# Delta layer of a two-layer decoder: GpSimd inverts blocks of 32 on 128 partitions, and one merging level fewer stays on TensorE

## The chip, the cores and the metric

The kernel runs on one core of a Trainium2 chip. The metric is the device time of one execution in microseconds (us), as the median of several executions. The profile is of one execution, taken by the hardware profiler.

## What is computed

Two layers over 1024 tokens of width 1024, each with a norm, one input projection, a mixer, a gate and one output projection. The change touches the mixer of the first layer only, a gated delta rule with 8 heads. The kernel works on chunks of 128 tokens (the reference on 64, with the same result). Cut to what matters:

```python
def gated_delta_rule(q, k, v, g, beta):
    ...
    lower = jnp.where(strict, jnp.einsum("bhnid,bhnjd->bhnij", k_beta, k) * decay, 0.0)
    rhs = jnp.concatenate([v * beta[..., None], k_beta * jnp.exp(g)[..., None]], axis=-1)
    sol = lax.linalg.triangular_solve(lower + jnp.eye(C, dtype=f32), rhs,
                                      left_side=True, lower=True, unit_diagonal=True)
    u, w = sol[..., :DV], sol[..., DV:]
    qk = jnp.einsum("bhnid,bhnjd->bhnij", q, k) * decay

    def step(state, inp):
        q_c, k_c, u_c, w_c, g_c, qk_c = inp
        v_new = u_c - jnp.einsum("bhck,bhkv->bhcv", w_c, state)
        o = (jnp.einsum("bhck,bhkv->bhcv", q_c * jnp.exp(g_c)[..., None], state)
             + jnp.einsum("bhij,bhjv->bhiv", qk_c, v_new))
        ...
```

The kernel needs the inverse of `lower + I` for each of the 8 chunks (tiles of 128x128) of each head.

## The kernel before

The delta layer is the function `delta_heads`. It runs a `body(m, n, p)` nine times: in each, head n is projected, convolved and prepared while head m = n - 1 goes through its merging levels and its chain of 8 states. The first body has no head m, the last one no head n. I number the bodies 0 to 8 by their n. A body is 36 slots, and each engine has its own program of the same slots, in order. On TensorE (PE) a slot s holds a piece of head m's chain, then 8 matmuls of 128x512 of the projection (`three_passes`, L373), then the small products of head n, and last the merging level of head m if there is one in this slot. In the last body only a part of a gate projection, 4 matmuls per slot, is left of the projection (`GATE_PARTS`).

The inverse of a tile is made in two ways. GpSimd (POOL) inverts the diagonal blocks of size BLK = 16 by forward substitution, all 64 blocks of a head at a time, a block on each partition (`invert_blocks`, L604 to L629): two instructions for each of 15 columns, a product (L619) and a subtraction (L622), each waiting for the one before. Then LEVELS = 3 merging levels join blocks of 16 to 32, 64 and 128. A level takes two slots of PE: in the first, two products `first` (L955), copied by ScalarE (ACT) to `bc` (L669); in the second, four products `lev` (L962, L964; two in the last level), applied by VectorE (DVE) to `zx1` (L1017) or, at the end, to `zf` (L1019). The four pairs of tiles start 6 slots apart, the first at slot LEVEL0 = 1. The masked inputs of all levels of a pair are made by one POOL instruction (`um`, L591).

The path of the blocks between layouts goes through DRAM, by DMAs that SyncE (SP) issues in its own order. At slot 21 (`BLOCKS_OUT`) SP stores the tiles u (L553), waits, and loads the blocks to `bd` (L557). At slot 34 (`INVERSE_BACK`) it waits for POOL (L564), stores the two results (L567, L568), waits for both (L569) and loads the four parts of `zx` (L572). The first two of these four hold the first pair of tiles, and PE waits for them at the first level of the next body (L952). In SP's order there follow the last store of head m's output (L562, slot 36) and, at slot 3 of the next body, the load of that head's second weight unit, 512 KB (L534). ACT waits for this load in its slot 2 (`split_high`, L639), ahead of its own later slots. In a body in which ACT also has the copy `bc` in slot 2, that copy stands ahead of `split_high`.

Of the kernel before, what the change touches and what calls it, by code (L numbers as in the profile page):

```python
# [25 lines left out]
P = 128  # L26
S = 1024
D = 1024
T = S // P
# [12 lines left out]
EXP_LN = "natural_log_exp_and_others"  # L42
BIG = 1e30
ARG_MAX = 44.0
BLK = 16
NB = P // BLK
LEVELS = 3
BLOCK_STEP = BLK * (P + 1)
TILE_STEP = NB * BLOCK_STEP

# [294 lines left out]
SLOTS = 36  # L345
UNITS = 6
HALVES = 2 * UNITS
LEVEL0 = 1
DECAYS = (12, 15)
CHAIN0 = 7  # L350
K_TURNS = (22, 34)
# [25 lines left out]
def delta_heads(nc, g, weights, proj, o_turned):  # L377
# [5 lines left out]
    with ExitStack() as ctx:  # L383
        m_ = Mem(nc, ctx, "a")
# [12 lines left out]
        cols = m_.sb("cols", [P, 7, T, H])  # L397
        hc = m_.sb("hc", [P, 2, 7, T])
        hw = m_.sb("hw", [P, 2, CONV, 4])
        bd = m_.sb("bd", [NB * T, BLK, BLK])  # L400
        bx = m_.sb("bx", [NB * T, BLK, BLK])
        bt = m_.sb("bt", [NB * T, (BLK // 2) ** 2])
        dec = m_.sb("dec", [P, T, P])
        um = m_.sb("um", [P, 2, LEVELS, P])
        bc = m_.sb("bc", [P, 2, P])
# [15 lines left out]
        u_dram = nc.dram_tensor("u_tiles", [T * TILE_STEP], F32, kind="Internal").ap()  # L421
        inv_dram = nc.dram_tensor("inverse_tiles", [2, T * TILE_STEP], F32, kind="Internal").ap()
# [5 lines left out]
        def as_blocks(flat):  # L428
            return (flat.rearrange("(p x) -> p x", x=BLOCK_STEP)[:, 0:BLK * P]
                    .rearrange("p (j i) -> p j i", i=P)[:, :, 0:BLK])  # L430

        step = m_.ps("step", [P, 2, DV])
        new = m_.ps("new", [P, DV])
# [18 lines left out]
        inv_out, inv_zero = sem("inv_out"), sem("inv_zero")  # L452
        back = [sem("back_first"), sem("back_rest")]
        bstep = sem("bstep")
# [73 lines left out]
        @block.sync  # L528
        def _(sp):
            def load(n, j):  # L530

                sp.wait_ge(w_low, n * UNITS + j)
                sp.sem_inc(carrier, 1)
                sp.dma_start(raw[:, slot_of(j)], weights.w[:, bass.ds(col_of(n, j), P)]  # L534
                             .rearrange("(k p) c -> p k c", p=P)).then_inc(w_landed[slot_of(j)], 16)


            sp.wait_ge(zx_zero, 1)
            for c in range(2):
                sp.dma_start(as_tiles(inv_dram[c]), zx[:, :, c, :]).then_inc(inv_zero, 16)  # L540
            sp.wait_ge(inv_zero, 32)

            def body(m, n, p):
                for s in range(DELAYED):
                    if n is not None and s < SLOTS and s % 6 == 3:
                        j = s // 6 + 1
                        if j < UNITS:
                            load(n, j)
                        elif not (isinstance(n, int) and n == H - 1):
                            load(n + 1, 0)  # L550
                    if n is not None and s == BLOCKS_OUT:
                        sp.wait_ge(ut, n * 4 + 2)
                        sp.dma_start(as_tiles(u_dram), u[:, :, :]).then_inc(blocks_out, 16)  # L553
                        if not (isinstance(n, int) and n == 0):
                            sp.wait_ge(inv_out, n * 32)
                        sp.wait_ge(blocks_out, n * 16 + 16)
                        sp.dma_start(bd[:, :, :], as_blocks(u_dram)).then_inc(blocks_in, 16)  # L557
                    if m is not None and (s - CHAIN0 - 8) % 3 == 0 and 0 <= (s - CHAIN0 - 8) // 3 < T:
                        t = (s - CHAIN0 - 8) // 3
                        sp.wait_ge(og_s, m * T + (t + 1 + T))  # L560
                        dst = o_turned[bass.ds(m * DV, DV), t * P:(t + 1) * P].rearrange("(c p) n -> p c n", p=P)
                        sp.dma_start(dst, og[:, :, :]).then_inc(o_stored, 16)  # L562
                    if n is not None and s == INVERSE_BACK:
                        sp.wait_ge(blocks_inv, n * 2 + 2)  # L564

                        sp.wait_ge(lv_s, n * (LEVELS * T // 2) + 1)
                        sp.dma_start(as_blocks(inv_dram[0]), bd[:, :, :]).then_inc(inv_out, 16)  # L567
                        sp.dma_start(as_blocks(inv_dram[1]), bx[:, :, :]).then_inc(inv_out, 16)  # L568
                        sp.wait_ge(inv_out, n * 32 + 32)  # L569
                        for part, tiles in enumerate((slice(0, 2), slice(2, T))):  # L570
                            for c in range(2):
                                sp.dma_start(zx[:, tiles, c, :], as_tiles(inv_dram[c])[:, tiles]  # L572
                                             ).then_inc(back[part], 16)

            heads(sp, body)
            sp.wait_ge(o_stored, 16 * (1 + H * T))

        @block.gpsimd
        def _(pool):
            pool.memset(zx[:, :, :, :], 0.0).then_inc(zx_zero, 1)  # L580
            pool.wait_ge(cols_s, 1)

            def body(m, n, p):
                if n is not None:
                    columns_and_taps(n, p)
                if m is not None:
                    for b in range(T // 2):

                        pool.wait_ge(first_mm, m * (LEVELS * T // 2) + (LEVELS * b + 1))
                        pool.wait_ge(ut, m * 4 + 2)  # L590
                        pool.tensor_tensor(um[:, :, :, :], spread(u[:, 2 * b:2 * b + 2, :], 2, LEVELS),  # L591
                                           spread(g.level_mask[:, :, :], 1, 2), ALU.mult).then_inc(um_s, 1)
                if n is not None:
                    invert_blocks(n)

            def columns_and_taps(n, p):

                pool.wait_ge(og_s, n * T)
                pool.tensor_copy(hc[:, p], cols[:, :, :, bass.ds(n, 1)].rearrange("p a t o -> p a (t o)")
                                 ).then_inc(hc_s, 1)  # L600
                for c, tile in ((0, n + H), (1, n + 0), (2, n * 2 + 2 * H), (3, n * 2 + (2 * H + 1))):
                    pool.tensor_copy(hw[:, p, :, c:c + 1], g.conv[:, :, bass.ds(tile, 1)]).then_inc(hc_s, 1)

            def invert_blocks(n):  # L604

                if not (isinstance(n, int) and n == 0):
                    pool.wait_ge(inv_out, n * 32)
                pool.sem_inc(carrier, 1)
                pool.memset(bx[:, :, :], 0.0).then_inc(bstep, 1)
                pool.wait_ge(bstep, n * (2 * BLK) + 1)  # L610
                pool.sem_inc(carrier, 1)
                pool.tensor_copy(bx[:, :, :].rearrange("t j i -> t (j i)")[:, 0:BLK * BLK:BLK + 1],
                                 g.ones[0:NB * T, 0:BLK]).then_inc(bstep, 1)
                pool.wait_ge(blocks_in, n * 16 + 16)
                for j in range(BLK - 1):
                    pool.wait_ge(bstep, n * (2 * BLK) + (2 + 2 * j))
                    rows, width = BLK - 1 - j, j + 1
                    prod = bt[:, 0:rows * width].rearrange("t (i c) -> t i c", c=width)
                    pool.tensor_tensor(prod, spread(bd[:, j, j + 1:BLK], 2, width),  # L619
                                       spread(bx[:, j, 0:width], 1, rows), ALU.mult).then_inc(bstep, 1)  # L620
                    pool.wait_ge(bstep, n * (2 * BLK) + (3 + 2 * j))
                    pool.tensor_tensor(bx[:, j + 1:BLK, 0:width], bx[:, j + 1:BLK, 0:width], prod,  # L622
                                       ALU.subtract).then_inc(bstep if j < BLK - 2 else blocks_inv, 1)

                pool.wait_ge(blocks_inv, n * 2 + 1)
                pool.sem_inc(carrier, 1)
                pool.tensor_copy(bd[:, :, :], bx[:, :, :].rearrange("t i c -> t c i")).then_inc(blocks_inv, 1)
                pool.wait_ge(blocks_inv, n * 2 + 2)
                pool.sem_inc(bstep, 1)  # L629

            heads(pool, body)

        @block.scalar
        def _(act):
# [26 lines left out]
            def body(m, n, p):  # L661
                pm = 1 - p
                for s in range(DELAYED):
                    if m is not None:
                        b, k = divmod(s - LEVEL0 - 1, 6)
                        if 0 <= b < T // 2 and k % 2 == 0:
                            use = LEVELS * b + k // 2
                            act.wait_ge(first_mm, m * (LEVELS * T // 2) + (use + 1 + 1))
                            act.activation(bc[:, :, :], first[:, :, :], ACT.Copy).then_inc(first_c, 1)  # L669
# [101 lines left out]
        def _(pe):  # L771
# [18 lines left out]
            def body(m, n, p):  # L790
# [23 lines left out]
                for s in range(SLOTS):  # L814
# [124 lines left out]
                    if m is not None:  # L939

                        b, k = divmod(s - LEVEL0, 6)
                        if 0 <= b < T // 2:
                            level, second = divmod(k, 2)
                            use = LEVELS * b + level
                            x = zx[:, 2 * b:2 * b + 2] if level == 0 else zx1[:, :, :, :]
# [24 lines left out]
        def _(dve):  # L970
# [33 lines left out]
            def body(m, n, p):  # L1004
                pm = 1 - p
                for s in range(DELAYED):
                    if m is not None:
                        b, k = divmod(s - LEVEL0 - 2, 6)
                        if 0 <= b < T // 2 and k % 2 == 0:
                            level = k // 2  # L1010
                            use = LEVELS * b + level
                            x = zx[:, 2 * b:2 * b + 2] if level == 0 else zx1[:, :, :, :]
# [1191 lines left out]
```

## Time and profile before

| | |
|---|---|
| median of 3 executions | 2395.16 us |
| the profiled execution | 2399.3 us |
| its span, first to last instruction | 2397.6 us |
| PE busy | 2308.8 us (96%) |
| PEld busy (weight loads, beside PE) | 1922.3 us (80%) |
| DVE busy | 1423.4 us (59%) |
| ACT busy | 1264.1 us (53%) |
| POOL busy | 245.5 us (10%) |

Busy times are sums over the whole span, so they don't say what bounds one stage. The delta layer takes the first 955 us of the span. All times in the rows further down are counted from the start of the span. In the timelines, an entry is start, duration, engine, line, operation, output<-input and a count, with idle time and its releaser in square brackets; consecutive matmuls overlap, so that the time a matmul costs is the distance to the start of the next, not its duration.

### The profile page before, as it was taken

Reading aid. Unit: us, or ns where it says so; the run is one execution under the profiler, and the core shown is the slowest. Engines: PE = TensorE matmul, PEld = TensorE weight load, DVE = VectorE, ACT = ScalarE, POOL = GpSimd, SP = SyncE. Lnnn points to the kernel's source line nnn. Section 1 sums busy time; section 2 is a strip of 40 time slices with the busy share of each in tenths; the row PEclk is TensorE's granted clock in tenths of the full one; section 3 lists DMA queues with packets and bytes.
Section 4 is the critical chain, followed back from the end, with each engine's and each line's share of the span. In section 5 each row is a group of like instructions: output and inputs, shape, how many; then the busy total and the mean of one; then the engine's idle time right before and its main releaser. Section 6 shows DMA issues by size and latency. Waiting matters only on the chain. (4 is left out here: it accounts for less than half of the span.)

```text
span 2397.6 us, 35088 instructions
## 1 busy us (share of the span) xinstructions
PE 2308.8 (96%) x11486; PEld 1922.3 (80%) x11486; DVE 1423.4 (59%) x2614; ACT 1264.1 (53%) x2565; POOL 245.5 (10%) x387
## 2 busy tenths in 40 slices
PE   7999999999999997999999999999999999999869
PEld 6788888887888876778788888888888888888757
DVE  5665756575757563786663827456382745638155
ACT  5556556565556654555445455454554445455433
POOL 1202121211212120830000000000000000000000
PEclk9999999999999999999999999999999999999989
DMA  4123030212121221978112112111211211111077
GB/s 135 38 58 79 23 88 24 78 37 66 39 62 50 54 63 30 292 265 283 54 28 63 36 35 70 35 53 32 56 35 35 70 35 53 38 51 36 19 240 268
DMA packets 279550, 186.26 MB, mean 78 GB/s; under 512 B 72140, under 2 KB 258660, under 8 KB 279428
## 3 DMA queue, kind: packets, MB, share of 16 engines
q1 hardware_dynamic: 279428, 184.73, 26.2%
q8 instruction: 65, 1.06, 0.2%
q14 instruction: 57, 0.47, 0.1%
HBM read 157.23 MB, written 27.46 MB: 77 GB/s over the span
## 5 line engine op out<-in xcount | busy, mean ns | idle before, releaser
L373 PE MATMUL b_front<-g_h_hi,wb_w_hi 128*128 128x512 f32 x1280 | 511.8, 400 | 3.0 <-PEq L1275 3.0
L373 PE MATMUL b_front<-g_h_hi,wb_w_lo 128*128 128x512 f32 x1280 | 511.4, 400 | 0.0
L373 PE MATMUL b_front<-g_h_lo,wb_w_hi 128*128 128x512 f32 x1280 | 510.3, 399 | 0.0
L373 PE MATMUL a_proj<-g_h_hi,wa_w_hi 128*128 128x512 f32 x784 | 323.3, 412 | 3.2 <-ACT a_acc L720 1.7
L373 PE MATMUL a_proj<-g_h_lo,wa_w_hi 128*128 128x512 f32 x784 | 323.0, 412 | 0.0
L373 PE MATMUL a_proj<-g_h_hi,wa_w_lo 128*128 128x512 f32 x784 | 316.8, 404 | 0.0
L373 PEld LDWEIGHTS b_front<-g_h_hi,wb_w_hi 128*128 128x128 f32 x1280 | 241.7, 189 | 51.6 <-issue 3.3
L373 PEld LDWEIGHTS b_front<-g_h_hi,wb_w_lo 128*128 128x128 f32 x1280 | 241.5, 189 | 50.6
L373 PEld LDWEIGHTS b_front<-g_h_lo,wb_w_hi 128*128 128x128 f32 x1280 | 241.7, 189 | 49.2
L1864 ACT ACTIVATE b_acc<-b_front,g_gains 128x512 f32<-128x512 f32 x96 | 66.2, 689 | 285.4 <-DVE b_qk L2123 206.0
L2020 DVE TENSOR_TENSOR wb_w_lo<-wb_raw,wb_w_hi 128x1024 fp32r<-128x1024 f32 x79 | 95.9, 1214 | 140.0 <-ACT wb_w_hi L1825 140.0
L373 PEld LDWEIGHTS a_proj<-g_h_hi,wa_w_hi 128*128 128x128 f32 x784 | 148.3, 189 | 33.9 <-issue 3.2
L373 PEld LDWEIGHTS a_proj<-g_h_lo,wa_w_hi 128*128 128x128 f32 x784 | 148.4, 189 | 29.8 <-issue 1.0
L373 PEld LDWEIGHTS a_proj<-g_h_hi,wa_w_lo 128*128 128x128 f32 x784 | 148.1, 189 | 27.9
L1080 DVE SCALAR_TENSOR_TENSOR a_acc<-a_x_raw,a_hw,a_acc 128x512 f32<-128x512 f32 x192 | 145.7, 759 | 6.8
L2088 DVE TENSOR_TENSOR b_sq_lo<-b_sg,b_sq_hi 128x512 fp32r<-128x512 f32 x96 | 66.2, 690 | 80.7 <-ACT b_sq_hi L1869 80.7
L591 POOL TENSOR_TENSOR a_um<-a_u,g_level_mask 128x768 f32<-128x768 f32 x32 | 60.9, 1902 | 426.8 <-PE a_first L955 426.6
L669 ACT ACTIVATE a_bc<-a_first 128x256 f32<-128x256 f32 x96 | 36.5, 380 | 127.6 <-PE a_first L955 119.1
L1017 DVE TENSOR_TENSOR a_zx<-a_zx,a_lev 128x512 f32<-128x512 f32 x64 | 43.9, 685 | 79.2 <-PE a_lev L964 79.2
L2123 DVE TENSOR_TENSOR b_qk<-b_acc,b_sg 128x512 f32<-128x512 f32 x96 | 90.0, 938 | 0.1
L725 ACT ACTIVATE a_sg<-a_sg 128x512 f32<-128x512 f32 x92 | 57.0, 620 | 56.2 <-DVE a_sg L1084 56.0
L1897 ACT ACTIVATE b_v<-b_side 128x512 f32<-128x512 f32 x48 | 28.6, 596 | 107.8 <-PE b_side L2006 107.8
(273 smaller groups left out, 4565.6 us busy)
## 6 DMA issues: line engine op xcount, KB each, us to landing
wb_raw<-in_b_w_in_dram SPq DMA_DIRECT2D x80, 512.0 KB, 3.9
p_w_raw<-in_a_w_out_dram SPq DMA_DIRECT2D x64, 512.0 KB, 4.2
wa_raw<-in_a_w_in_dram SPq DMA_DIRECT2D x48, 512.0 KB, 4.2
p_w_raw<-in_b_w_out_dram SPq DMA_DIRECT2D x32, 512.0 KB, 4.2
a_out<-a_og SPq DMA_DIRECT2D x64, 128.0 KB, 1.8
p_a_raw<-a_out SPq DMA_DIRECT2D x64, 128.0 KB, 5.1
a_zx<-inverse_tiles SPq DMA_DIRECT2D x16, 384.0 KB, 4.5
u_tiles<-a_u SPq DMA_DIRECT2D x8, 512.0 KB, 3.2
```

The lines of the kernel that those rows point to most:

```text
L373: last = pe.matmul(out, w[:, k, :], a[:, k, ks], start=(n == 0), stop=(n == 23))
L591: pool.tensor_tensor(um[:, :, :, :], spread(u[:, 2 * b:2 * b + 2, :], 2, LEVELS), spread(g.level_mask[:, :, :], 1, 2), ALU.mult).then_inc( ...
L669: act.activation(bc[:, :, :], first[:, :, :], ACT.Copy).then_inc(first_c, 1)
L725: act.activation(sg[:, q % 2], sg[:, q % 2], ACT.Exp).then_inc(sigs, 1)
L1017: dve.tensor_tensor(zx1[:, :, :, :], x, lev[:, :, :, :], ALU.subtract).then_inc(lv_s, 1)
L1080: ins = dve.scalar_tensor_tensor(acc[:, half], src, w, acc[:, half], ALU.mult, ALU.add)
L1864: act.activation(acc[:, half], proj[half][:, :], ACT.Copy, scale=r.gains[:, gain:gain + 1]).then_inc(rope, 1)
L1897: act.activation(v[:, c // 2, (c % 2) * TH:(c % 2 + 1) * TH, :], side[:, :].rearrange("p (t c) -> p t c", t=TH), ACT.Copy).then_inc(v_kept, 1)
L2020: dve.tensor_tensor(w_lo[slot_of(j)][:, :, :], raw[:, slot_of(j)], w_hi[slot_of(j)][:, :, :].bitcast(F32), ALU.subtract).then_inc(w_low, 1)
L2088: dve.tensor_tensor(sq_lo[:, :], sg[:, q % 2], sq_hi[:, :].bitcast(F32), ALU.subtract).then_inc(sq_low, 1)
L2123: dve.tensor_tensor(out, a, b_, ALU.mult).then_inc(qkn, 1)
```

## The change

BLK goes from 16 to 32 and LEVELS from 3 to 2: POOL inverts 32 blocks of 32 per head, and the level that joined 16 to 32 is gone. To use all 128 partitions, the columns of a block's inverse are dealt to four groups of 32 partitions, 8 columns (`PART`) to each; `bd` is loaded four times, once for each group. The substitution has 31 columns instead of 15, with a width of at most 8. The results are stored by eight DMAs instead of two. LEVEL0 goes from 1 to 3: a pair's levels take slots 3 to 6 of its six instead of 1 to 6, so that the last level stays where it was.

```diff
-BLK = 16
+BLK = 32
 NB = P // BLK
-LEVELS = 3
+LEVELS = 2
+PARTS_OF_BLOCK = P // BLK
+PART = BLK // PARTS_OF_BLOCK
...
-LEVEL0 = 1
+LEVEL0 = 3
...
-        bd = m_.sb("bd", [NB * T, BLK, BLK])
-        bx = m_.sb("bx", [NB * T, BLK, BLK])
-        bt = m_.sb("bt", [NB * T, (BLK // 2) ** 2])
+        bd = m_.sb("bd", [P, BLK, BLK])
+        bx = m_.sb("bx", [P, BLK, PART])
+        bt = m_.sb("bt", [P, (BLK - PART) * PART])
+        bxt = bd[:, 0:PART, :]
...
+        def part_of(tile, q):
+
+            return tile[q * NB * T:(q + 1) * NB * T]
+
+        def columns(q):
+            return slice(q * PART, (q + 1) * PART)
...
-                        sp.dma_start(bd[:, :, :], as_blocks(u_dram)).then_inc(blocks_in, 16)
+                        for q in range(PARTS_OF_BLOCK):
+                            sp.dma_start(part_of(bd, q), as_blocks(u_dram)).then_inc(blocks_in, 16)
...
-                        sp.dma_start(as_blocks(inv_dram[0]), bd[:, :, :]).then_inc(inv_out, 16)
-                        sp.dma_start(as_blocks(inv_dram[1]), bx[:, :, :]).then_inc(inv_out, 16)
-                        sp.wait_ge(inv_out, n * 32 + 32)
+                        for q in range(PARTS_OF_BLOCK):
+                            sp.dma_start(as_blocks(inv_dram[1])[:, :, columns(q)], part_of(bx, q)).then_inc(inv_out, 16)
+                            sp.dma_start(as_blocks(inv_dram[0])[:, columns(q)], part_of(bxt, q)).then_inc(inv_out, 16)
+                        sp.wait_ge(inv_out, (n + 1) * (32 * PARTS_OF_BLOCK))
...
-                pool.tensor_copy(bx[:, :, :].rearrange("t j i -> t (j i)")[:, 0:BLK * BLK:BLK + 1],
-                                 g.ones[0:NB * T, 0:BLK]).then_inc(bstep, 1)
-                pool.wait_ge(blocks_in, n * 16 + 16)
+                for q in range(PARTS_OF_BLOCK):
+                    diag = part_of(bx, q)[:, columns(q), :].rearrange("t i c -> t (i c)")[:, 0:PART * PART:PART + 1]
+                    ins = pool.tensor_copy(diag, part_of(g.ones, q)[:, 0:PART])
+                ins.then_inc(bstep, 1)
+                pool.wait_ge(blocks_in, (n + 1) * (16 * PARTS_OF_BLOCK))
                 for j in range(BLK - 1):
                     pool.wait_ge(bstep, n * (2 * BLK) + (2 + 2 * j))
-                    rows, width = BLK - 1 - j, j + 1
+                    rows, width = BLK - 1 - j, min(j + 1, PART)
...
-                pool.tensor_copy(bd[:, :, :], bx[:, :, :].rearrange("t i c -> t c i")).then_inc(blocks_inv, 1)
+                pool.tensor_copy(bxt, bx[:, :, :].rearrange("t i c -> t c i")).then_inc(blocks_inv, 1)
...
-                        if 0 <= b < T // 2:
+                        if 0 <= b < T // 2 and k < 2 * LEVELS:
                             level, second = divmod(k, 2)
```

ACT's and DVE's parts of the levels are cut in the same way.

## Rows read from the trace of the kernel before

**Rows 1.** Windows, one period: length, busy of PE, PEld, DVE, ACT, POOL; clock, DMA share, GB/s

```profile
120.00:230.60 110.60, 110.26 (x588) 92.96 (x587) 69.92 (x128) 63.90 (x138) 19.12 (x37) 1.00 0.21 54
```

**Rows 2.** Timeline of PE, slots 1 to 3 of body 2

```profile
237.37 0.40 PE L373 MATMUL a_proj<-g_h_hi,wa_w_hi 128*128 128x512 f32 x1
237.60 0.61 PE L955 MATMUL a_first<-a_zx,a_um 128*128 128x128 f32 x4
...
242.65 0.61 PE L955 MATMUL a_first<-a_zx,a_um 128*128 128x128 f32 x4
```

**Rows 3.** Timeline of POOL, the inversion of body 1 and the next um

```profile
197.17 0.21 POOL L619 TENSOR_TENSOR a_bt<-a_bd,a_bx 64x15 f32<-64x15 f32 x1 [14.13 <-DMA a_bd<-u_tiles]
197.46 0.22 POOL L622 TENSOR_TENSOR a_bx<-a_bx,a_bt 64x15 f32<-64x15 f32 x1
...
198.28 0.72 POOL L622 TENSOR_TENSOR a_bx<-a_bx,a_bt 64x28 f32<-64x28 f32 x1
...
204.07 0.31 POOL L622 TENSOR_TENSOR a_bx<-a_bx,a_bt 64x64 f32<-64x64 f32 x1
...
211.00 1.02 POOL L627 COPY a_bd<-a_bx 64x256 f32<-64x256 f32 x1 [0.17 <-POOL a_bx L622]
...
231.68 1.85 POOL L591 TENSOR_TENSOR a_um<-a_u,g_level_mask 128x768 f32<-128x768 f32 x1
```

**Rows 4.** Groups of DVE, 197.1 to 210.9: count | busy us, mean ns | idle

```profile
L1080 DVE SCALAR_TENSOR_TENSOR a_acc<-a_x_raw,a_hw,a_acc 128x512 f32<-128x512 f32 x6 | 4.5, 752 | 0.2
L1078 DVE TENSOR_SCALAR a_acc<-a_x_raw,a_hw 128x512 f32<-128x512 f32 x2 | 1.0, 478 | 0.0
L1091 DVE TENSOR_TENSOR a_acc<-a_acc,a_sg 128x512 f32<-128x512 f32 x1 | 0.7, 681 | 0.0
L1084 DVE TENSOR_SCALAR a_sg<-a_acc 128x512 f32<-128x512 f32 x1 | 0.4, 426 | 0.0
```

**Rows 5.** The same groups of DVE, 199.2 to 235.5

```profile
L1080 DVE SCALAR_TENSOR_TENSOR a_acc<-a_x_raw,a_hw,a_acc 128x512 f32<-128x512 f32 x5 | 3.8, 752 | 0.2
L1084 DVE TENSOR_SCALAR a_sg<-a_acc 128x512 f32<-128x512 f32 x6 | 2.8, 474 | 0.8 <-ACT a_acc L720 0.7
L1095 DVE SCALAR_TENSOR_TENSOR a_z<-a_acc,g_gains,a_sg 128x512 f32<-128x512 f32 x3 | 2.7, 894 | 1.2 <-ACT a_sg L729 1.2
L973 DVE TENSOR_TENSOR wa_w_lo<-wa_raw,wa_w_hi 128x1024 fp32r<-128x1024 f32 x2 | 2.4, 1220 | 1.0 <-ACT wa_w_hi L639 1.0
L1091 DVE TENSOR_TENSOR a_acc<-a_acc,a_sg 128x512 f32<-128x512 f32 x2 | 1.4, 683 | 0.0
L1078 DVE TENSOR_SCALAR a_acc<-a_x_raw,a_hw 128x512 f32<-128x512 f32 x1 | 0.5, 477 | 0.0
```

**Rows 6.** Timeline of SP's DMA issues, bodies 1 and 2

```profile
193.75 0.63 SPq L557 DMA_DIRECT2D a_bd<-u_tiles  x1
...
226.77 0.67 SPq L568 DMA_DIRECT2D inverse_tiles<-a_bx  x1
229.42 2.00 SPq L572 DMA_DIRECT2D a_zx<-inverse_tiles  x4
...
232.39 0.38 SPq L534 DMA_DIRECT2D wa_raw<-in_a_w_in_dram  x1
```

**Rows 7.** DMA issues of 225 to 240: count, KB each, median us to landing

```profile
wa_raw<-in_a_w_in_dram SPq DMA_DIRECT2D x2, 512.0 KB, 6.1
```

**Rows 8.** Body 0 and start of body 1: timelines of SP and of PE

```profile
97.78 0.70 SPq L557 DMA_DIRECT2D a_bd<-u_tiles  x1
...
127.01 0.60 PE L955 MATMUL a_first<-a_zx,a_um 128*128 128x128 f32 x4
```

**Rows 9.** Body 7 and start of body 8: timelines of POOL and of PE

```profile
864.43 0.21 POOL L619 TENSOR_TENSOR a_bt<-a_bd,a_bx 64x15 f32<-64x15 f32 x1 [13.60 <-DMA a_bd<-u_tiles]
...
894.17 1.13 PE L955 MATMUL a_first<-a_zx,a_um 128*128 128x128 f32 x4 [1.81 <-DMA a_zx<-inverse_tiles]
```

**Rows 10.** Windows, columns as in Rows 1, after PE stood still for 11 us

```profile
964.00:965.00 1.00, 1.00 (x4) 0.71 (x4) 0.94 (x1) 1.00 (x2) 0.00 (x0) 0.50 1.19 291
```

More of the change, by code:

```diff
@@ L554, in body @@
                         if not (isinstance(n, int) and n == 0):
-                            sp.wait_ge(inv_out, n * 32)
+                            sp.wait_ge(inv_out, n * (32 * PARTS_OF_BLOCK))
                         sp.wait_ge(blocks_out, n * 16 + 16)
-                        sp.dma_start(bd[:, :, :], as_blocks(u_dram)).then_inc(blocks_in, 16)
+                        for q in range(PARTS_OF_BLOCK):
+                            sp.dma_start(part_of(bd, q), as_blocks(u_dram)).then_inc(blocks_in, 16)
                     if m is not None and (s - CHAIN0 - 8) % 3 == 0 and 0 <= (s - CHAIN0 - 8) // 3 < T:
@@ L606, in invert_blocks @@
                 if not (isinstance(n, int) and n == 0):
-                    pool.wait_ge(inv_out, n * 32)
+                    pool.wait_ge(inv_out, n * (32 * PARTS_OF_BLOCK))
                 pool.sem_inc(carrier, 1)
@@ L665, in body @@
                         b, k = divmod(s - LEVEL0 - 1, 6)
-                        if 0 <= b < T // 2 and k % 2 == 0:
+                        if 0 <= b < T // 2 and k in range(0, 2 * LEVELS, 2):
                             use = LEVELS * b + k // 2
@@ L1008, in body @@
                         b, k = divmod(s - LEVEL0 - 2, 6)
-                        if 0 <= b < T // 2 and k % 2 == 0:
+                        if 0 <= b < T // 2 and k in range(0, 2 * LEVELS, 2):
                             level = k // 2
```

## Prediction

> **What bounds the kernel now.** I read the windows first. In a period of the delta layer, PE is busy 110.26 of 110.60 us at the full clock [rows 1]; seven bodies (1 to 7) look like this, a little shorter in the last. So what leaves PE there shortens the kernel, as long as nothing that PE waits for comes later than now. POOL, with 19.1 us busy in the period, seems to have room, but that is an average: what counts is when its result is wanted. So the second view was the timeline of each engine around the inversion, from the issue of the block load at 193.75 to the first level of the next body at 237.60 [rows 2, 3, 6].
>
> **What PE gains.** Between the `first` products of two levels lie 5.05 us, two slots [rows 2]. They hold 16 projection matmuls, which cost 0.23 us each (237.37 to 237.60 [rows 2]), 3.66 us in all. A level costs 1.39 us: 12 records, 4 of them `first`, so 0.46 for those. The change takes out one level of 4 pairs in 8 heads: 32 x 1.39 = 44.5 us. ACT and DVE lose 32 small instructions each, and um gets a third shorter; these ran beside PE and are worth nothing. At the end of the last body PE is not full, so part of its 5.6 us may not be had.
>
> **What POOL gets.** Now 30 instructions with 1360 elements per partition, then 62 with 6312: sum over j of (31-j) x min(j+1, 8), twice. Clean ones take 0.31 us for 64 elements and 1.85 for 768 [rows 3]: 2.2 ns an element and 0.16 us fixed, and 0.08 lies between two (197.17 + 0.21 to 197.46 [rows 3]). So 62 x 0.24 + 6312 x 0.0022 = 28.8 us clean. With the slope between 15 and 64 elements (0.21 to 0.31; 0.0016 to 0.0020) it would be about 27: the lower bound. I take 28.8, since most instructions have 100 to 192 elements, and the slope to 768 covers that size.
>
> They won't be clean. By the same prices the present inversion would take 10.2 us, but it took 13.7 (197.17 to 211.00 less 0.17 [rows 3]): 3.5 more. A subtraction of 28 elements took 0.72 us while DVE ran L1080, all of whose operands are in SBUF [rows 3, 4]. DVE's instructions of this kind were busy 6.6 us there [rows 4], so each of their microseconds costs POOL 0.53. In the time in which the new inversion would run they are busy 13.6 us [rows 5]: 7.2 more. T = 36.0 us. For the first and last inversion I take 5 instead of 7.2, as less of the convolution lies beside them: T = 33.8. The Trainium skill ("SBUF — State Buffer", section "SBUF: two separate sides") says that VectorE and GpSimd share a port pair as an exclusive lock, and that the loser is blocked for the whole instruction. The row with 0.72 us agrees in kind. By the full rule, not 0.53 but nearly all of the 13.6 us would be lost; that is a rival below.
>
> **The path around it.** The chain from the block load to the first level is now: 3.4 us from issue at 193.75 to POOL's start [rows 3, 6], the inversion, the copy, the stores, the loads. The pieces change so. Four block loads instead of one: 3 more issues of 0.63 to 0.70 [rows 6, 8], +2.0; POOL starts 5.4 after the first. The copy has the same 256 elements: 0.17 + 0.8, between the 1.02 in the row [rows 3] and a clean one; 1.0. The stores: eight issues. The four of single columns have 1024 pieces each, as many as today's block store (0.67 [rows 6]); for the four others with a quarter of the pieces I take 0.45. The last is issued 4.5 us after the first, and the wait ends about 3.1 later (2.65 now, 226.77 to 229.42 [rows 6]): 7.6. This is the least sure piece, as pieces of 32 bytes occur nowhere in the trace: between 6.5 and, if they cost the DMA engines twice as much, 11.6. The zx loads stay.
>
> Then comes what stands behind SP's wait for POOL. The weight load of the next body is issued 3.0 us after the first zx load (229.42 to 232.39) and took 6.1 to land, beside the zx traffic [rows 6, 7]. ACT waits for it in its slot 2. The first `bc` copy moves from slot 2 to slot 4, behind this wait; ACT has three instructions from there (the split, one evacuation, the copy), for which I take 2.0. PE needs `bc` at the end of slot 4. In sum, PE's `lev` can start at X + 5.4 + T + 1.0 + 7.6 + 3.0 + 6.1 + 2.0 = X + T + 25.1, X being the issue of the block load.
>
> PE would be there, undisturbed, at 237.60 + 3.66 (slots 2 and 3, now empty) + 0.46 + 1.83 = 243.55. What lies between slot 21 and the end of the body is as long as before: there the change swaps a first level for a last one only in name. That the three extra issues delay the store of head m's output, and DVE and PE by up to 2 us in slot 22, costs nothing as long as PE has to wait for the inversion anyhow.
>
> **The sum.** Bodies 2 to 7: 193.75 + 36.0 + 25.1 = 254.85 against 243.55, a stall of 11.3 us. After a stand of 11 us PE ran at 0.50 of its clock (1.2 instead of 2.4 GHz), with 4 matmuls per us [rows 10], for about 3 us, which costs about 1.3. So 12.6, six times: 75.6.
> Body 1: 97.78 + 33.8 + 25.1 - 0.6 (no output store) = 156.1, against 127.01 + 3.66 + 2.29 = 132.96 [rows 8]: 23.1 + 1.3 = 24.4.
> Body 8 has no weight load. POOL starts at 864.43 + 2.0, and the zx data land at + 33.8 + 1.0 + 7.6 + 2.8 = 911.6. PE reached this point at 892.36 and waited 1.81 [rows 9]; two short slots later, at 894.2, it would now wait 17.4, + 1.3 = 18.7, and the 1.81 are gone.
> 75.6 + 24.4 + 18.7 - 1.8 - 44.5 = +72.4 us. The profiled execution took 2399.3 us, 4.1 above the median of the runs: it would become 2471.7, and the median 2467.6.
>
> **The rivals.**
> *The inversion keeps up* (the other side). What speaks for it: POOL is 90% idle, and its instructions with an inner width of 8 are more regular than today's. Each us of T counts 8 times, so the balance is at T = 27, 9 us below my value, which is the clean time without any lock. At T = 25 the stalls of bodies 2 to 7 all but vanish; bodies 1 and 8 keep 13 and 8: 2395 - 46 + 21 + 2 = 2372. The 3.5 us lost in the present inversion speak against it.
> *Only the zx data are waited for*, and the weight load comes in time. Then PE waits at slot 3: 193.75 + 5.4 + 36.0 + 8.6 + 2.6 = 246.4 against 241.3, 5.1 + 1.3, six times; body 1 18.8, body 8 18.7: 2395 + 38 + 19 + 19 - 46 = 2425. Against it: the order of SP's issues is fixed, and the load landed at 238.5, with no slack to speak of.
> *The lock takes all*: T = 42.4 in bodies 2 to 7 and some 4 more in the others: +6.4 x 6 + 8 = 2514. For it: longer instructions of POOL also hold DVE up, which the short ones of today do not. L1095 has a mean of 894 ns [rows 5].
> *Small pieces are dear*: stores + 4 us, eight times: 2500.
>
> **Chances.** My forecast, T and the stores within 3 us of their values, 0.66; all lost to the lock or the dear stores, 0.16; only zx, 0.08; the inversion keeps up, 0.06; a balance within 0.2% by chance, 0.04. 0.2% (5 us) is about what a measurement of this kernel can tell from no change. Faster 0.07, same 0.03, slower 0.90. T between 31 and 40 and stores of 6.5 to 10 give 2422 to 2517; the range is 2422 to 2518, which takes in the zx case and most of the dearer ones.
>
> **What would show it.** Right: PE idle once in each of bodies 1 to 8, released in 1 to 7 by ACT's `bc` and ahead of it ACT by the DMA of wa_raw; SP waiting for POOL's copy some 11 us in each body; an inversion of 34 to 38 us; `lev` and `first` records down by a third or more; periods of about 117.6 us instead of 110.6. Wrong: an inversion under 28 us; or DVE's instructions visibly longer beside POOL, and PE waiting for DVE in slots 22 to 35.

## The result, and the profile after

The kernel after takes 2509.1 us (median of 4 runs) against 2394.4 for the kernel before beside it: ratio 1.0475, 95% interval 1.0448 to 1.0503, 114.7 us slower. The forecast was 2467.6 (2422 to 2518). The direction is right and the time lies in the range, but the size is short by 42 us: +114.7 instead of +72.4. Where these come from is the larger part of what follows.

Windows over two bodies of the delta layer, as in [rows 1] (length, busy of PE, PEld, DVE, ACT, POOL; clock, DMA share, GB/s):

```profile
220.00:337.20 117.20, 107.96 (x537) 89.07 (x535) 69.82 (x125) 62.96 (x134) 38.24 (x78) 0.96 0.23 57
337.20:454.50 117.30, 106.88 (x525) 87.77 (x524) 67.20 (x120) 63.62 (x135) 34.86 (x72) 0.96 0.23 56
```

A body takes 117.2 us instead of 110.6. PE stands idle for 9 to 10 of them, and is busy for 107 although its work shrank by 5, since it runs at half its clock for a while behind the longest stand. This is that stand, at the start of body 2 (timelines of POOL, SP, PE and ACT; they answer to [rows 2, 3, 6]):

```profile
216.79 0.24 POOL L633 TENSOR_TENSOR a_bt<-a_bd,a_bx 128x31 f32<-128x31 f32 x1 [15.75 <-DMA a_bd<-u_tiles]
...
251.57 0.66 POOL L641 COPY a_bd<-a_bx 128x256 f32<-128x256 f32 x1 [0.17 <-POOL a_bx L636]
```

```profile
211.22 2.61 SPq L568 DMA_DIRECT2D a_bd<-u_tiles  x4
...
252.34 0.33 SPq L579 DMA_DIRECT2D inverse_tiles<-a_bx  x1
...
256.89 0.56 SPq L580 DMA_DIRECT2D inverse_tiles<-a_bd  x1
258.82 1.99 SPq L584 DMA_DIRECT2D a_zx<-inverse_tiles  x4
261.07 0.38 SPq L573 DMA_DIRECT2D a_out<-a_og  x1
261.78 1.74 SPq L544 DMA_DIRECT2D wa_raw<-in_a_w_in_dram  x2
```

```profile
261.54 0.71 PE L969 MATMUL a_first<-a_zx,a_um 128*128 128x128 f32 x4 [0.49 <-DMA a_zx<-inverse_tiles]
269.68 0.80 PE L976 MATMUL a_lev<-a_zx,a_bc 128*128 128x128 f32 x2 [5.60 <-ACT a_bc L683]
...
272.41 0.63 PE L375 MATMUL a_proj<-g_h_hi,wa_w_hi 128*128 128x512 f32 x1
272.84 0.63 PE L375 MATMUL a_proj<-g_h_lo,wa_w_hi 128*128 128x512 f32 x1
```

```profile
267.81 1.06 ACT L653 ACTIVATE wa_w_hi<-wa_raw 128x1024 fp32r<-128x1024 f32 x1 [10.47 <-DMA wa_raw<-in_a_w_in_dram]
269.25 0.38 ACT L683 ACTIVATE a_bc<-a_first 128x256 f32<-128x256 f32 x1
```

The inversion runs from 216.79 to 251.40. Its eight stores keep SP busy to 257.4, then come the zx loads, and only at 261.78 the weight load. ACT waits for that, and with it `bc`; PE waits for `bc`. The matmuls behind it start 0.43 us apart instead of 0.23: PE is at 1.2 of its 2.4 GHz (the granted clock is 0.50 in each of the windows of 1 us from 267 to 273, and 0.81 on average from 257 to 275). This is the chain of the prediction, link by link.

PE's longest waits over the delta layer (us in all, times, longest):

```profile
PE a_lev L976 <- ACT a_bc L683: 29.8, 9, 5.6
PE a_first L969 <- DMA a_zx<-inverse_tiles: 28.6, 5, 14.3
PE a_turn L909 <- DVE a_og L1059: 23.7, 8, 4.2
```

The third, at the K turn (the transposition of K's tiles on PE), was not priced. DVE's `og` waits for the store of the `og` before it, which SP issues in slot 21 behind the four block loads, and the K turn on PE waits for the `turn` buffer. The prediction named this delay and put it at nothing, as long as PE had to wait for the inversion anyhow.

**Where the 114.7 us are.** Landmarks of the two traces give the split. The eighth inversion starts at 864.43 before and at 923.77 after, 59.3 us later. The first matmul of the delta layer's output projection starts at 962.66 before and at 1028.22 after: +65.6. The last `ln_row` load of the attention layer is issued at 2282.22 before and at 2391.77 after: +109.6. So 44 us arise in the attention layer, in which the diff touches nothing, and some 5 behind it, which I have not followed. Its `ln_row` loads, one per head, are 139.5 us apart on average before and 145.8 after. DVE's waits over the kernel after, and its timeline where the loop over heads begins anew:

```profile
DVE b_swap L2116 <- issue: 41.8, 6, 7.7
```

```profile
1442.97 0.69 DVE L2102 TENSOR_TENSOR b_sq_lo<-b_sg,b_sq_hi 128x512 fp32r<-128x512 f32 x1 [1.32 <-ACT b_sq_hi L1883]
1443.59 0.01 DVE L2114 LOAD_MASK_SELECT b_swap<-b_acc  x1
1443.59 0.72 DVE L2114 STREAM_SHUFFLE b_swap<-b_acc 32x512 f32<-32x512 f32 x1
1450.78 0.68 DVE L2116 TENSOR_TENSOR b_swap<-b_swap,t_sin 32x512 f32<-32x512 f32 x1 [6.46 <-issue]
```

DVE stands 6.5 us here (7.7 at most) between two instructions, released by nothing but its own issue, and does so six times: once per iteration but the first. PE waits in turn for what DVE hands on:

```profile
PE b_ring L1956 <- DVE b_qk L2137: 34.8, 6, 6.5
```

The page's rows of the instruction queues, first those of before, then those of after:

```profile
q8 instruction: 65, 1.06, 0.2%
q14 instruction: 57, 0.47, 0.1%
```

```profile
q8 instruction: 62, 1.02, 0.2%
q14 instruction: 89, 0.73, 0.1%
```

q14 moved 32 packets of 8 KB more, although there are fewer instructions. In the attention layer's loop before, it has none from 1400 to 2150; after, 5 in each iteration. This suggests that DVE's code of this loop, 282 instructions, is fetched anew in each iteration after and was not before. The change takes 44 instructions out of DVE's program ahead of it: counted in the built programs, the loop starts at instruction 1250 before and at 1206 after.

### The profile page after: what moved, and what is told of

It is laid out like the page before. It is cut to its first block and busy times, and to the rows that moved or that the text cites. A ratio compares the mean times of both kernels' runs of the same rounds, so it can differ in the third digit from the quotient of the medians.

```text
span 2511.7 us, 34672 instructions
## 1 busy us (share of the span) xinstructions
PE 2313.2 (92%) x11102; PEld 1912.2 (76%) x11102; DVE 1410.3 (56%) x2582; ACT 1251.6 (50%) x2533; POOL 380.4 (15%) x664
## 5 line engine op out<-in xcount | busy, mean ns | idle before, releaser
L375 PE MATMUL a_proj<-g_h_lo,wa_w_hi 128*128 128x512 f32 x784 | 328.7, 419 | 0.0
L375 PE MATMUL a_proj<-g_h_hi,wa_w_lo 128*128 128x512 f32 x784 | 322.7, 412 | 0.0
L375 PEld LDWEIGHTS a_proj<-g_h_hi,wa_w_hi 128*128 128x128 f32 x784 | 151.6, 193 | 33.8 <-issue 4.4
L633 POOL TENSOR_TENSOR a_bt<-a_bd,a_bx 128x112 f32<-128x112 f32 (+29 forms) x248 | 112.2, 452 | 180.4 <-DMA a_bd<-u_tiles 161.6
L636 POOL TENSOR_TENSOR a_bx<-a_bx,a_bt 128x112 f32<-128x112 f32 (+29 forms) x248 | 123.8, 499 | 19.4
L1956 PE MATMUL b_ring<-b_qk 128*128 128x128 f32 (+1 forms) x384 | 81.1, 336 | 34.8 <-DVE b_qk L2137 34.8
L987 DVE TENSOR_TENSOR wa_w_lo<-wa_raw,wa_w_hi 128x1024 fp32r<-128x1024 f32 x47 | 58.9, 1253 | 93.7 <-ACT wa_w_hi L653 93.7
L603 POOL TENSOR_TENSOR a_um<-a_u,g_level_mask 128x512 f32<-128x512 f32 x32 | 41.4, 1294 | 437.8 <-PE a_first L969 437.5
L1956 PEld LDWEIGHTS b_ring<-b_qk 128*128 128x128 f32 x384 | 66.4, 201 | 46.7 <-issue 37.3
```

What stands on the lines that cost most here:

```text
L375: last = pe.matmul(out, w[:, k, :], a[:, k, ks], start=(n == 0), stop=(n == 23))
L987: dve.tensor_tensor(w_lo[slot][:, :, :], raw[:, slot], w_hi[slot][:, :, :].bitcast(F32), ALU.subtract).then_inc(w_low, 1)
L1956: mm = pe.matmul(ring[i % 3][:, c * 2 * P:c * 2 * P + width], qk[:, 2 * g, first:first + P], qk[:, 2 * g + 1, begin:begin + width], start= ...
```

## The experiments

### Does the place of the code make the stalls?

All four kernels add semaphore increments that move no data. Each ratio here and below is to the kernel before on the same chip.

```diff
                           (p_kept[1], 1), (o_stored, 16)):
                 dve.sem_inc(s_, c)
+            for _ in range(44):
+                dve.sem_inc(carrier, 1)
```

**a_pad44**, the kernel after:

> The changed kernel with 44 VectorE instructions (semaphore increments, no data) put ahead of the attention layer's loop over heads, so that this loop stands at the same place of VectorE's instruction stream as in the kernel before (instruction 1250 of the built program instead of 1206). Theory of placement: the loop of 282 VectorE instructions is fetched anew in each iteration only where it straddles one block of instructions too many; with its old place the six stalls of 6.5 to 7.7 us before the multiplication of b_swap go, and with them about 46 us: 2463 us (2458 to 2470), 139.5 us per head in the attention layer. Rival, the stalls come from elsewhere (addresses of tiles, memory state, what the delta layer leaves): 2509 to 2513, the stalls stay.

Measured: ratio 1.0313 (1.0293 to 1.0333). The six stalls are gone. The expected times were for a chip on which the kernel before takes 2395 us; as ratios they are 1.026 to 1.031, and the measured one stands at their upper end. The `ln_row` loads are 141.1 us apart, and 140.9 in b_act45 on the same chip, which has the attention layer of before: nothing of the stalls is left in it. **a_pad8**, with 8 in place of 44:

> The changed kernel with only 8 such instructions ahead of the attention loop (loop at 1214). The stall falls 5 or 6 instructions behind the loop's start, so the theory of placement says that the block's boundary lies there: 8 instructions more push the whole loop behind it and the stalls go as with 44: about 2463 us. If the boundary is not there but the place matters some other way (alignment of the loop's start, a boundary elsewhere), the stall moves or stays: 2490 to 2513. Rival without placement: 2509.

Measured: 1.0288 (1.0265 to 1.0311). At the loop's jump DVE goes on without a stand:

```profile
1448.51 0.75 DVE L2116 STREAM_SHUFFLE b_swap<-b_acc 32x512 f32<-32x512 f32 x1
1449.29 0.68 DVE L2118 TENSOR_TENSOR b_swap<-b_swap,t_sin 32x512 f32<-32x512 f32 x1
```

Eight instructions do what 44 do. The two ratios can hardly be told apart, though the 44 cost a stand of 5.9 us of their own on DVE, and the eight none (in that trace ACT stands once on issue, for 4.6 us):

```profile
DVE wb_w_lo L2036 <- issue: 5.9, 1, 5.9
```

**b_pad212**, the kernel before with 212 in the same place:

> The kernel before with 212 VectorE semaphore increments ahead of the attention loop: loop at 1462, which is 256 more than its place in the changed kernel. Theory of placement with blocks of 256 instructions: the stalls appear in the kernel before, at the same multiplication, six times 6.5 to 7.7 us, with about 46 us more plus up to 12 us once for the 212 instructions themselves: 2441 to 2455. Rival without placement: 2395 to 2407.

Measured: 1.0305 (1.0288 to 1.0321), that is 73 us on the 2406.8 of the kernel before on that chip. DVE's waits:

```profile
DVE b_swap L2104 <- issue: 49.4, 6, 9.1
DVE wb_w_lo L2022 <- issue: 21.4, 1, 21.4
```

The stalls appear at the same instruction of the kernel before, and q14 has the same 89 packets. The 212 instructions cost 21.4 instead of at most 12, and the stalls are up to 9.1 us there: my range was too low, the place of the code as the cause is shown. The stall hangs on the loop's start: 1206 and 1462 = 1206 + 256 have it; 1214 and 1250 don't. A boundary that repeats every 256 instructions and lies within the first eight behind 1206 explains all four: with it the loop touches three blocks at the two slow places and two at the others. The Trainium skill ("Runtime: NRT & Kernel Launch", section "Instruction fetch mechanics") says that instructions are fetched in blocks of 16 KiB, 256 of them, that two blocks are held, and that a jump back out of these two waits for the fetch. The four starts agree, and so does the place of the stand, in front of the loop's seventh instruction. The size of a block does not show as clearly: the packets on q14 are of 8 KB, and five of them make 40 KB in an iteration.

**b_act45**, the kernel before with 45 increments on ACT ahead of the delta layer, which puts its loop 44 instructions further on in the built program (from 147 to 191):

> The kernel before with 44 more ScalarE instructions (semaphore increments) ahead of the delta layer's loop over pairs of heads. In the kernel before, ScalarE's loop of 496 instructions stalls twice (4.6 and 4.0 us, on nothing but issue) at its jump back, VectorE's loop, as long, does not and starts at 185 instead of 147; moved to 191 ScalarE's should stay clear as well. Placement: the two stalls go, 2391 us (2389 to 2394). Rival (a jump back costs this wherever the loop stands): 2395 to 2398.

Measured: 1.0004 (0.9993 to 1.0015), and both stands are still there:

```profile
ACT a_bc L671 <- issue: 9.9, 2, 5.3
```

A miss. This loop has 496 instructions; by the rule of two blocks only 17 of 256 places would be free of the stand, and I had taken ACT's offset from DVE's. Whether such a place exists was not tried. My premise, that DVE's loop of the same length has no stand, was not shown either: at the jump DVE waits for PE anyway, and a fetch behind such a wait does not show. The kernel after is a case of this. Its ACT loop, 477 instructions from 147, shows no wait on issue, since ACT waits for the weight load at the jump; in a44_load below, where that load comes earlier, the stand is there, twice. These are the jump of before on DVE and that of a44_load on ACT:

```profile
354.02 0.69 DVE L1017 TENSOR_TENSOR a_zx<-a_zx,a_lev 128x512 f32<-128x512 f32 x1 [5.44 <-PE a_lev L964]
```

```profile
368.82 1.06 ACT L657 ACTIVATE wa_w_hi<-wa_raw 128x1024 fp32r<-128x1024 f32 x1 [2.42 <-issue]
```

### What sets the period in the delta layer?

These stand on a_pad44, so that the attention layer runs as before; 1.0313 is their point of comparison. **a44_half** does 15 of the 31 steps and leaves out the rest, so that its inverse is unfinished; it serves for the time alone. In a_pad44, PE waits so:

```profile
PE a_lev L976 <- ACT a_bc L683: 29.7, 9, 5.4
PE a_first L969 <- DMA a_zx<-inverse_tiles: 28.1, 4, 14.4
PE a_turn L909 <- DVE a_og L1059: 24.5, 7, 4.5
```

The edit:

```diff
-                for j in range(BLK - 1):
+                for j in range(STEPS):
```

> The changed kernel with the 44 VectorE instructions of a_pad44 (so that the attention layer runs as before), and of the inversion's 31 steps only the first 15: the substitution is left unfinished, the output is not the reference's, every other instruction stands. T falls from 34.7 us to 335.23 -> 353.90 = 18.7 us and the copy. Theory: the 82 us of first, lev and K-turn waits of the padded kernel come from the inversion's length (first and lev, 58 us and the half clock behind them) and from SP's queue (K turn, 24.5 us); the first two vanish and the gain of 32 TensorE stages (44.5 us) comes out: ratio to the kernel before 0.990 to 1.000 (K turn and its clock, some 30 us, stay). Rival, the removed levels save less than their 1.39 us each, or the stall hangs on the DMAs and not on the substitution: 1.005 or above.

Measured: 1.0021 (1.0010 to 1.0031), a little above the expected range. `first` and `lev` waits fall from 57.8 to 13.5 us, but the K turn stays at 24.5 and eats most of the gain. **a44_half_og** takes that away too, by a move on SP: in slot 21 the store of `og` is issued ahead of the store and the loads of the blocks.

```diff
+                    if m is not None and (s - CHAIN0 - 8) % 3 == 0 and 0 <= (s - CHAIN0 - 8) // 3 < T:
...
                     if n is not None and s == BLOCKS_OUT:
                         sp.wait_ge(ut, n * 4 + 2)
```

> a44_half (15 of the inversion's 31 steps, unfinished inverse, output not the reference's) with the store of og in slot 21 ahead of the loads of u's blocks. In a44_half the K turn still waits 24.5 us and TensorE runs at the half clock behind it; with no inversion wait left to take its place, this time must come out: ratio 0.985 to 0.989 against 1.002, inversion starts about 105 us apart. It measures what one body of TensorE's work takes with two levels instead of three: 104.8 us if a stage costs the 1.39 us of the prediction. Rival, a stage costs less on an otherwise full TensorE: 107 us or more and a ratio of 0.993 or above.

Measured: 0.9893 (0.9876 to 0.9909). One period, with PE full:

```profile
202.20:307.40 105.20, 104.75 (x538) 87.25 (x537) 68.20 (x125) 63.27 (x136) 24.43 (x45) 1.00 0.26 62
```

This period is 105.2 us against 110.6: the level is worth 5.4 of the 5.6 predicted. From the second inversion to the eighth the periods average 106.5 against 111.2, as a `lev` wait of up to 5.0 us is left in places. **a44_og** is the same move with the full inversion:

> The padded kernel with the store of og in slot 21 issued on SP ahead of the store and the four loads of u's blocks instead of behind them. The K-turn waits of TensorE (24.5 us, up to 4.5 us a body) then go. Theory, the chain of the inversion sets the period and the K turn stands beside it: first and lev wait longer by as much, the ratio stays at 1.028 to 1.031. Rival, stalls add up: 24.5 us and their clock go, ratio 1.018 to 1.021.

Measured: 1.0254 (1.0236 to 1.0273), between the two. PE's waits over the kernel:

```profile
PE a_first L969 <- DMA a_zx<-inverse_tiles: 51.7, 8, 15.8
PE a_lev L976 <- ACT a_bc L683: 25.0, 9, 4.0
...
PE a_turn L909 <- DVE a_og L1059: 0.4, 1, 0.4
```

The K turn's 24.1 us went, and `first` and `lev` wait 18.9 us longer. Three quarters of the wait were only moved. So the K turn stands beside the inversion's chain and not in it, as the first theory had it, but not wholly: 14 us came out (1.0313 to 1.0254), more than the 5 that the waits show. What makes up the rest is open; the half clock behind the third stand is a candidate, since the mean clock rose from 0.968 to 0.971. **a44_load** issues the next weight load ahead of SP's wait for POOL:

```diff
-                        if j < UNITS:
+                        if j == 1 and m is not None:
+                            pass
+                        elif j < UNITS:
                             load(n, j)
...
                     if n is not None and s == INVERSE_BACK:
+                        if not (isinstance(n, int) and n == H - 1):
+                            load(n + 1, 1)
                         sp.wait_ge(blocks_inv, n * 2 + 2)
```

> The padded kernel with the next head's second weight load issued on SP ahead of the wait for the inversion instead of behind it. Theory of the prediction: the lev stall (5 us a body) is this load, late behind the inversion's eight stores; without it only the load of zx is waited for, the chain inversion start -> zx landed (46.7 us) -> first -> next inversion start (65.4 us) sets a period of about 112 instead of 117.2 us: ratio 1.018 (1.012 to 1.022) against 1.031 of the padded kernel. Rival, weight load and zx are equally late: 1.028 to 1.031. Rival, the weight load was the whole stall: 1.008 or less.

Measured: 1.0110 (1.0093 to 1.0127), just below the expected range:

```profile
PE a_first L973 <- DMA a_zx<-inverse_tiles: 27.7, 4, 16.2
PE a_turn L913 <- DVE a_og L1063: 23.3, 8, 4.6
...
PE a_lev L980 <- ACT a_bc L687: 0.6, 2, 0.3
```

The `lev` waits go from 29.7 to 0.6 and nothing takes their place. 49 us came out (1.0313 to 1.0110), more than these 29; the half clock behind those waits is again a candidate, as the mean clock rose from 0.968 to 0.979. The last link of the chain in the prediction, zx issue to weight load to ACT to `bc`, was the one that ended last.

### A version that is faster than both

**v2** makes both moves and stores the inverse of the first two tiles first, so that their zx loads are issued 4.5 us behind the first store (465.05 to 469.52) instead of 6.5:

```diff
                         for part, tiles in enumerate((slice(0, 2), slice(2, T))):
+                            rows = slice(tiles.start * NB, tiles.stop * NB)
+                            for q in range(PARTS_OF_BLOCK):
+                                sp.dma_start(as_blocks(inv_dram[1])[rows, :, columns(q)],
+                                             part_of(bx, q)[rows]).then_inc(inv_out, 16)
+                                sp.dma_start(as_blocks(inv_dram[0])[rows, columns(q)],
+                                             part_of(bxt, q)[rows]).then_inc(inv_out, 16)
+                            sp.wait_ge(inv_out, n * (64 * PARTS_OF_BLOCK) + (part + 1) * (32 * PARTS_OF_BLOCK))
                             for c in range(2):
```

> Both moves together, and the inverse stored in two parts: the eight pieces of the first two tiles first, then their load into zx, then the other six tiles. Store to zx issue should fall from 8 us to about 4. Theory of the chain: period 46.7 - 3.5 + 65.4 = 108.6 us, ratio 1.003 to 1.010; were the chain short enough to be hidden, 1.000 or below.

Measured: 0.9992 (0.9982 to 1.0003), the kernel before's time. The inversions start 106.8 to 109.1 us apart from the second on, 107.8 on average, near the chain's 108.6; the ratio came out below the range. Some 4 us of that lie in the attention layer, whose loads are 138.8 us apart here and 139.4 in the other runs on this chip, which I have not followed. **v3** shortens the chain at its head: u's second half one slot earlier on PE and ahead of the convolution on DVE, and the four stores of `bx` ahead of POOL's last copy.

```diff
-K_GRAMS = (16, 19)
+K_GRAMS = (16, 18)
...
-                        sp.wait_ge(blocks_inv, n * 2 + 2)
+                        sp.wait_ge(blocks_inv, n * 2 + 1)
```

> v2 with two more cuts in the chain that sets its period (inversion start to inversion start, 107 to 109 us in v2): the second half of u is made one slot earlier on TensorE and ahead of the convolution's taps on VectorE (in v2 it is done at 421.0 though the chain could have it at about 416.6: 4 us less), and the four pieces that don't need POOL's last copy are stored ahead of it (0.9 us less). Theory of the chain: its length falls to about 103.5 us, below TensorE's own work (before's 110.35 - 4 x 1.39 = 104.8 us a body), which takes over: inversion starts 105 to 105.5 us apart, ratio to the kernel before 0.985 to 0.990. Rival, VectorE's taps come later by what u takes ahead of them and TensorE waits for them: 0.993 to 1.000.

Measured: 2368.6 us, ratio 0.9885 (0.9868 to 0.9901). Its periods:

```profile
307.80:413.70 105.90, 105.27 (x540) 87.44 (x539) 69.53 (x125) 63.58 (x135) 37.81 (x77) 1.00 0.27 64
413.70:518.60 104.90, 104.57 (x539) 87.38 (x538) 68.60 (x125) 63.46 (x135) 37.95 (x78) 1.00 0.27 63
```

In these bodies PE is full again, with the whole inversion in its shadow. It still waits for it in body 1 and body 8, 8.5 and 11.5 us:

```profile
PE a_first L979 <- DMA a_zx<-inverse_tiles: 20.0, 2, 11.5
```

So blocks of 32 with this order are worth 1.2% (of which some 5 us lie in the attention layer again: 138.8 us a head against 139.6 in a44_half_og on this chip); as the change was made, its chain stretched a body to 117.2 us instead of 105. The moves alone were not tried on the kernel before; in its bodies 2 to 7 PE has no wait of more than 1.0 us that they could take away.

## Why the prediction was right or wrong

- **PE's gain, 32 x 1.39 = 44.5 us.** Nearly right: 5.4 of 5.6 us in a body in which nothing else stands in the way (a44_half_og), and 5.7 on average over the six periods of v3 (105.5 against 111.2). The records of `first` fell from 384 to 256.
- **T = 36.0 us.** Measured 34.3 to 34.6 in bodies 1 to 6 (216.79 to 251.40 in body 1), 34.2 and 33.1 in the first and last, where 33.8 stood. The shortest time seen for each of the 62 instructions adds up to 24.2 us, and the gaps to 4.8: 29.0 clean, against 28.8. What DVE takes is therefore 5.6, not 7.2. DVE's groups in those 34.6 us:

```profile
L1094 DVE SCALAR_TENSOR_TENSOR a_acc<-a_x_raw,a_hw,a_acc 128x512 f32<-128x512 f32 x6 | 4.9, 810 | 0.2
L987 DVE TENSOR_TENSOR wa_w_lo<-wa_raw,wa_w_hi 128x1024 fp32r<-128x1024 f32 x2 | 2.8, 1384 | 0.9 <-ACT wa_w_hi L653 0.9
L1098 DVE TENSOR_SCALAR a_sg<-a_acc 128x512 f32<-128x512 f32 x5 | 2.5, 496 | 0.1
L1105 DVE TENSOR_TENSOR a_acc<-a_acc,a_sg 128x512 f32<-128x512 f32 x2 | 1.6, 792 | 0.0
L1109 DVE SCALAR_TENSOR_TENSOR a_z<-a_acc,g_gains,a_sg 128x512 f32<-128x512 f32 x2 | 1.6, 778 | 1.2 <-ACT a_sg L743 1.2
```

  With L1092 (1.2) they are busy 14.6 us, so each of their microseconds cost POOL 0.38, where I had 0.53 from short instructions. They lengthen too: L987 has 1384 ns against 1220 in [rows 5]. The rival in which the lock takes all is out, and with it the size, not the kind, of the rule on the shared port pair that the prediction took from the Trainium skill ("SBUF — State Buffer", section "SBUF: two separate sides"): a microsecond of DVE's cost POOL 0.38 here, not 1.
- **The pieces of the path.** Block loads to POOL's start 5.6 us (5.4). The copy 0.17 + 0.66 (1.0). Stores to zx issue 6.5 (7.6), and 5.6 to 8.2 over the bodies, so pieces of 32 bytes did not cost what the upper bound of 11.6 allowed for. zx issue to weight load 3.0 (3.0). ACT's three instructions, 267.81 to 269.68, 1.9 (2.0). PE's `lev` came 269.68 - 211.22 = 58.5 us behind the block load, where T + 25.1 with T = 36.0 gives 61.1.
- **Bodies 2 to 7.** Forecast: 12.6 us of stall less 5.6 a body, a period of 117.6. Measured: 117.2, 120.5, 117.3, 119.5, 116.4, 116.0, against 110.1 to 113.1 before. PE does not wait once, for 11.3, but in three places, 2.7, 0.5 and 5.6 us in body 1 and 2. The six are 39.7 us longer than before, where 42 was forecast. The K turn that I put at nothing is one of the three places, and the run that takes its wait away is 14 us shorter over the whole kernel (a44_og). So the good agreement is in part two errors that cancel: a term left out, and a chain that came out shorter than priced.
- **The clock.** The prediction reads 4 matmuls per us from [rows 10]. That is the number of records that touch the window; their starts are 0.43 us apart, 2.3 per us, as the 0.50 says. The sum is not touched: it takes 3 us at half clock, and the trace of before shows 0.43 us between starts from 963.25 to 965.81.
- **Body 1.** The second inversion starts 116.35 us behind the first, against 96.14: +20.2, where 24.4 - 5.6 = 18.8 was forecast.
- **Body 8.** 65.6 - 59.3 = +6.3 us against 18.7 - 1.8 - 5.6 = 11.3. This is the term that was mis-sized:

```profile
966.12 1.22 PE L969 MATMUL a_first<-a_zx,a_um 128*128 128x128 f32 x4 [10.19 <-DMA a_zx<-inverse_tiles]
```

  PE waits 10.2 us, not 17.4. The zx data come 42.3 us behind the inversion's start, not 45.2 (T, stores and copy each a little shorter), and PE comes 32.2 us behind it, not 27.8, since it waited 4.5 us in the K turn before.
- **The delta layer in all:** +65.6 us in the trace against +72.4; with the attention layer's loop moved back (a_pad8, a_pad44), 2.9 to 3.1% for the whole kernel, that is +69 to +75. That the measured 2509 us lie in the range is luck: the range was made for a longer T and dearer stores, neither of which came, and was filled by 45 us from another layer.
- **The step that failed** is none of the sum but its frame. The sum adds stalls and gains of the delta layer to the time before, with no term for the rest: I took all else to keep its time and did not look at the attention layer. The 45 us in it come from a change of place that the diff makes by taking out instructions, and no row of the delta layer could have shown them. The trace of before had a sign, though: ACT waits 8.6 us in 2 places on nothing but issue, at the delta loop's jump.
- **The rivals.** "Only zx is waited for" was built in a44_load: 1.011, where its 2425 us are 1.0125 times the kernel before. "The inversion keeps up" fell with T; its own balance, T = 27, holds only while the path around T stays as long. v3 hides T = 34 us by making that path shorter.

## What to carry to other kernels

A result that is handed over late is a chain; price it from the engine that makes its input to the engine that needs its output, with every DMA issue that stands in SP's order between, and look first at what of it can be issued earlier: here a few DMA issues and one product moved earlier in their engines' order turned +3% into -1.2%. Before believing a loss or a gain of a few per cent, compare the time per iteration in the stages that the change does not touch, and look for an engine that waits on issue alone (a wait for another engine at the same place hides it): eight idle instructions ahead of a loop were worth 1.9% here.

## What was not expected of the hardware

- A loop over heads of 282 VectorE instructions stalled up to 7.7 and 9.1 us in each iteration but the first at starts 1206 and 1462, and not at all at 1214 and 1250. In the first of them PE stands for 5.3 us and is then at half clock, 0.43 us between matmuls: the 9.3 us of the stand and what follows show a granted clock of 0.72.

```profile
1450.70:1460.00 9.30, 4.17 (x12) 3.50 (x13) 5.40 (x10) 0.00 (x0) 0.00 (x0) 0.72 0.21 58
```

- Semaphore increments on VectorE are not free in number: 44 in a row cost 5.9 us, 212 cost 21.4, some 0.1 us each. How much of it is instruction fetch, the rows don't show.
- A PE stand of 5.6 us is followed by some 4 us of work at 1.2 instead of 2.4 GHz (0.43 us between matmuls from 270.27 to 273.69), as one of 11 us did in the trace of before [rows 10].
